# Expert stage of a two-layer decoder kernel: four experts' outputs side by side, weights applied to the output, routing by sort and search

## The reference

```python
def hier_moe_block(x, norm_g, w_rg, b_rg, w_re, b_re, w1, w3, w2):
    xn = rms_norm(x, norm_g).reshape(n_tok, d)                      # 256 tokens x 1024
    g_prob = softmax(xn @ w_rg + b_rg);  g_w, g_idx = top_k(g_prob, 1)          # 1 of 4 groups
    e_logits = (xn @ w_re + b_re).reshape(n_tok, N_GROUPS, EXPERTS_PER_GROUP)
    e_in = take_along_axis(e_logits, g_idx)                         # that group's 8 logits
    e_w, e_idx = top_k(softmax(e_in), 2)                            # 2 of 8 experts
    e_w = e_w / sum(e_w) * g_w
    combine = zeros((n_tok, 32)).at[token, g_idx * 8 + e_idx].add(e_w)
    hid = silu(einsum("nd,edf->nef", xn, w1)) * einsum("nd,edf->nef", xn, w3)   # f = 256
    hid = hid * combine[:, :, None]
    return x + einsum("nef,efd->nd", hid, w2)
```

## Time and profile before

| | |
|---|---|
| median of 3 runs (lowest, highest) | 1025.53 us (1025.33, 1029.95) |
| the profiled execution, its span | 1027.59 us, 1025.6 us |
| PE busy | 965.9 us, 94% |
| DVE, ACT busy | 479.1 us (47%), 466.2 us (45%) |
| DMA | 293.36 MB, mean 286 GB/s |
| TensorE's granted clock, mean | 0.982 of full speed |

### The profile page before, as it was taken

How to read it: one execution, slowest core, us unless ns; L and a number is a source line. 1 busy time by engine, 2 the same in 40 slices (tenths; PEclk the granted TensorE clock), 3 DMA queues, 4 the chain that set the end, 5 groups by cost and what they waited for, 6 DMA issues and landing times.

```text
span 1025.6 us, 19125 instructions
## 1 busy us (share of the span) xinstructions
PE 965.9 (94%) x8018; PEld 784.6 (76%) x8018; DVE 479.1 (47%) x811; ACT 466.2 (45%) x719; POOL 23.7 (2%) x42
## 2 busy tenths in 40 slices
PE   7999999999999999977999999999999899999676
PEld 7898899899886666643598988998998866666344
DVE  6446775567753222211273577654587532222112
ACT  6455555565544333311275464564655443343111
POOL 1010000000000000000000100000000000000000
PEclk9999999999999999988999999999999999999899
DMA  9634544556898999999975246535668799999996
GB/s 301 239 123 164 171 165 164 206 179 233 316 358 313 404 421 419 420 420 420 391 254 177 83 164 187 189 125 205 246 209 358 296 356 408 420 420 420 420 420 255
DMA packets 85478, 293.36 MB, mean 286 GB/s; under 512 B 16976, under 2 KB 17040, under 8 KB 60816
## 3 DMA queue, kind: packets, MB, share of 16 engines
q1 hardware_dynamic: 85392, 292.12, 74.7%
HBM read 291.05 MB, written 1.05 MB: 285 GB/s over the span
## 4 chain that ended last, share of the span: by engine, by line
PE 79%; DMA 11%; DVE 4%; ACT 3%; issue 1%; SPq 1%; POOL 0%; DVEq 0%; ACTq 0%
PE ps_a L775 10%; PE ps_a L777 10%; PE ps_a L776 10%; PE ps_b L1099 8%; DMA units_over_splits<-in_w_dram 8%; PE ps_b L1119 5%; PE ps_a L759 5%; PE ps_b L1178 4%; PE ps_a L761 4%; PE ps_a L760 4%; PE ps_a L1162 4%; DMA units_over_branches<-in_w_dram 3%; PE ps_b L1048 2%; PE ps_b L986 1%; PE ps_b L878 1%
## 5 line engine op out<-in xcount | busy, mean ns | idle before, releaser
L1210 ACT ACTIVATE w_high<-weight_ring 128x1024 fp32r<-128x1024 f32 x166 | 174.8, 1059 | 206.0 <-PE ps_a L777 146.5
L1496 DVE TENSOR_TENSOR w_low<-weight_ring,w_high 128x1024 fp32r<-128x1024 f32 x168 | 202.9, 1225 | 127.2 <-ACT w_high L1210 124.2
L775 PE MATMUL ps_a<-xnT_high,w_high 128*128 128x256 f32 x704 | 201.5, 286 | 1.7 <-DVE xnT_low L1502 1.7
L777 PE MATMUL ps_a<-xnT_high,w_low 128*128 128x256 f32 x704 | 199.5, 283 | 0.0
L776 PE MATMUL ps_a<-xnT_low,w_high 128*128 128x256 f32 x704 | 198.5, 282 | 0.0
L775 PEld LDWEIGHTS ps_a<-xnT_high,w_high 128*128 128x128 f32 x704 | 133.4, 189 | 4.3 <-issue 4.3
L776 PEld LDWEIGHTS ps_a<-xnT_low,w_high 128*128 128x128 f32 x704 | 133.8, 190 | 0.5 <-issue 0.5
L777 PEld LDWEIGHTS ps_a<-xnT_high,w_low 128*128 128x128 f32 x704 | 132.5, 188 | 0.0
L1872 DVE TENSOR_TENSOR y_lo<-ps_b,y_hi 128x512 fp32r<-128x512 f32 x64 | 44.2, 691 | 150.6 <-ACT y_hi L1461 148.6
L1422 ACT ACTIVATE h<-ps_b 128x512 f32<-128x512 f32 x64 | 38.3, 598 | 125.3 <-PE ps_b L1099 125.3
L1178 PEld LDWEIGHTS ps_b<-fold,h 128*128 128x128 f32 x512 | 69.2, 200 | 33.0 <-issue 28.0
(11 more groups left out here) (343 smaller groups left out, 1568.7 us busy)
## 6 DMA issues: line engine op xcount, KB each, us to landing
weight_ring<-in_w_in_dram SPq DMA_DIRECT2D x64, 1024.0 KB, 5.4
units_over_splits<-in_w_dram SPq DMA_DIRECT2D x60, 1024.0 KB, 23.7
units_over_attention<-in_w_dram SPq DMA_DIRECT2D x46, 1024.0 KB, 15.8
weight_ring<-in_w_dram SPq DMA_DIRECT2D x40, 1024.0 KB, 20.7
units_over_branches<-in_w_dram SPq DMA_DIRECT2D x30, 1024.0 KB, 18.6
weight_ring<-in_w_branch_dram SPq DMA_DIRECT2D x12, 1024.0 KB, 5.2
unit_over_gates<-in_w_dram SPq DMA_DIRECT2D x10, 1024.0 KB, 17.9
weight_ring<-in_w_out_dram SPq DMA_DIRECT2D x8, 1024.0 KB, 6.6
```

What stands on the lines that cost most here:

```text
L775: mm(dst, wh, xh, start=row == 0 and s % 2 == 0, stop=False, skip_group_check=True)
L777: last = mm(dst, wl, xh, start=False, stop=row == rows - 1, skip_group_check=True)
L1210: A(mix_buf(whi, i), mix_raw(i), ACT.Copy).then_inc(hi_ready, 1)
L1496: v.tensor_tensor(mix_buf(wlo, i), mix_raw(i), mix_buf(whi, i).bitcast(F32), ALU.subtract).then_inc(lo_ready, 1)
```

## The change

- A group for `outputs` and `scatter` is now four experts. The 128 rows are 4 experts x 32 slots, and the two halves of the contraction are summed in PSUM by a second matmul. It is still 16 matmuls of 32 rows a group, so half as many per expert, and 8 for the scatter. Only the last two groups are pairs as before.
- `select` holds each expert's columns once. `selectT` has four places.
- The slots' weights are one column per group (`ws`), made with matmuls of one column, and are applied as ACT copies `y_hi` and as DVE makes `y_lo`. The multiplication in `hT` goes.
- The list is written by expert. w2 units come four at a time.
- The ring has 19 places, 2 serve once.
- Routing finds each group's eight logits sorted (`max`) and their places (`max_index`), for one tile at a time; the first tile's part is placed earlier.

```diff
+GROUPS = [(e, 4, 1) for e in range(0, NE - 4, 4)] + [(NE - 4, 2, 2), (NE - 2, 2, 2)]
-ONCE_UNITS = (4, 5, 9)
+ONCE_UNITS = (9, 5)
-    t.once = [once_y[:, :], once_XT1[:, :], once_selT[:, :]]
+    t.once = [once_y[:, :], once_XT1[:, :]]
-    t.ring += [split_[i] for i in (0, 3, 1, 4, 2, 5)]
+    t.ring += [split_[0], split_[3], split_[1], split_[4], unit_inputs[:, :], split_[2], split_[5]]
...
+    for e in range(NE):
+        g = GROUP_OF[e]
+        hidden(e)
+        if e == 0:
+            steps.append(("first", 0))
+            selecting.extend((1, piece, 0) for piece in range(2))
+        elif e == 1:
+            steps.append(("first", 1))
+        elif coming and (e % BATCH >= 2 or e % BATCH == 1 and coming[0][0] == BATCHES - 1):
+            gather()
+        if e == 2:
+            steps.append(("first_selT", 0))
+        if e % 4 == 0 and e:
+            outputs(g - 1)
+        elif e % 4 == 1 and e > 4:
+            steps.append(("scatter", GROUP_OF[e - 4]))
+        elif e == NE - 1:
+            outputs(LAST - 1)
+        hidden_T(e)
+        if e == NE - 1:
+            steps.append(("scatter", LAST - 1))
+        select_next()
+    outputs(LAST)
+    steps.append(("scatter", LAST))
...
+            if g == LAST - 1:
+                idle_work(11)
+            for i in range(count):
+                arrived(pe, n + i)
...
+                for turn_j in range(2 // cuts):
+                    for c in range(TILES):
+                        e, j = c // cuts, c % cuts + turn_j
+                        w2 = unit_buf(n + e)[:, j * D + n2 * 512:j * D + (n2 + 1) * 512]
+                        ins = mm(ps_y[c * SLOTS:(c + 1) * SLOTS, n2, :], t.hid[:, (first + e) % 4, j, :], w2,
+                                 start=turn_j == 0, stop=turn_j == 2 // cuts - 1, skip_group_check=True)
...
+                        A(t.yhi[:, n2 * 512:(n2 + 1) * 512], ps_y[:, n2, :], ACT.Copy,
+                          scale=t.ws[:, g:g + 1]).then_inc(yhi_done, 1)
...
+            for g in range(NG):
+                last = v.max(t.tops[:, tt, g, :], rest[:, tt, g, :])
...
+            for g in range(NG):
+                last = v.max_index(t.top_at[:, tt, g, :], t.tops[:, tt, g, :], rest[:, tt, g, :])
```

More of the change, by code:

```diff
@@ L64, with steps_of @@
 TOKEN_MAJOR = {"sbv", "mlv", "mbv", "mbq", "mbk", "if"}
-STEPS = [("rows", q) for q in range(NK // 2)] + [("weights", 0)] + [("select", q) for q in range(2)]
+def steps_of(n):
+    groups = [g for g, (e, _, _) in enumerate(GROUPS) if e // BATCH == n]
+    return ([("rows", q) for q in range(NK // 2)] + [("weights", groups)] +
+            [("select", groups[i:i + 2]) for i in range(0, len(groups), 2)])
 def bc(ap, axis, count):
@@ L486, in hidden_T, with outputs @@
         h_used.append(banks)
[L488 to L493, removed]
-    def gather():
[L497 to L504, removed]
+    def outputs(g):
+        first, count, _ = GROUPS[g]
+        steps.append(("y", (g, len(order))))
+        order.extend(("w2", e) for e in range(first, first + count))
+        used.extend(count * [used[-1] + TILES])
+        y_used.append(used[-1])
+    selecting, y_used = [], []
+    coming = [(n, i, step) for n in range(1, BATCHES) for i, step in enumerate(steps_of(n))]
+    def gather():
+        nonlocal banks
+        n, i, step = coming.pop(0)
+        steps.append(("gather", (n, *step, banks)))
+        banks += 1
+        if i == len(steps_of(n)) - 1 and n + 1 < BATCHES:
+            selecting.extend((n + 1, piece, banks) for piece in range(2))
     def select_next():
@@ L508, in select_next @@
             steps.append(("selection", selecting.pop(0)))
[L510 to L513, removed]
+    for e in range(NE):
+        g = GROUP_OF[e]
+        hidden(e)
+        if e == 0:
             steps.append(("first", 0))
-            selecting.extend((1, piece, 0) for piece in range(3))
-        else:
+            selecting.extend((1, piece, 0) for piece in range(2))
+        elif e == 1:
+            steps.append(("first", 1))
+        elif coming and (e % BATCH >= 2 or e % BATCH == 1 and coming[0][0] == BATCHES - 1):
             gather()
[L518 to L528, removed]
-            steps.append(("first_selT", 0))
[L530 to L536, removed]
+        if e == 2:
+            steps.append(("first_selT", 0))
+        if e % 4 == 0 and e:
[7 more added lines that the diff above has]
+            steps.append(("scatter", LAST - 1))
         select_next()
-    outputs(PAIRS - 1)
-    steps.append(("scatter", PAIRS - 1))
-    assert gathers == (BATCHES - 1) * len(STEPS) and not selecting
+    outputs(LAST)
+    steps.append(("scatter", LAST))
+    assert not coming and not selecting
     ONCE, RING = len(t.once), len(t.ring)
@@ L1813, in first_rows @@
                     ins.then_inc(rows_dve, 1)
-        select(0, 0)
+        select(0)
         low(1)
@@ L1845, in run_vector @@
                     if piece == 0:
-                        dve.wait_ge(*((given, uses) if uses else (first_given, 3)))
-                    if piece < 2:
-                        select(n, piece)
+                        dve.wait_ge(*((given, uses) if uses else (first_given, 2)))
+                        select(n)
                     else:
```

255 lines of the change are left out of this document (114 added, 141 removed).

## The result

| | before | after |
|---|---|---|
| median (lowest, highest), 20 runs each | 1027.42 us (1025.33, 1031.45) | 1031.78 us (1027.92, 1036.74) |
| ratio, 95% interval | | 1.0039 (1.0023 to 1.0054) |
| profiled execution, its span | 1027.59, 1025.6 us | 1031.16, 1029.2 us |
| PE busy | 965.9 us | 939.6 us |

The changed kernel is slower by 0.4%, though PE has 26 us less to do. The prediction was 5.6 us faster.

A forecast was written before the change was run, and what follows sets the result against it. The 420 GB/s weight stream was taken to bound the expert stages. Routing 0.6 plus start 2.6 gave 3.2 us a layer, 6.4 for two, less 0.8 at the end: 5.6 gained, median 1019.9 us, range 1016 to 1026.

The forecast's parts named there:

- What bounds the kernel: Expert stages: the weight stream at 420 GB/s, 2.50 us per unit, sets the stage; 75 streamed units take 187 us.
- PE's work per expert: Expert chain on PE: falls from 1.91 to 1.52 us per unit, worth nothing past 345 us, something at the start.
- Routing: Logits to the end of `assigned`: 2.7 us for 3.32, 0.6 us less a layer; bounds 1.0 less to 1.0 more.
- Start of the stream: First refills of each layer: twelfth lands at 35.5 for 38.5 us, 3.0 sooner; 2.6 us a layer taken.
- The ring: Ring of 19 places for 18: at worst 17 are held, so the DMA isn't stopped; 0 us.
- Output scale: ACT's and DVE's instructions per half keep their size and lie beside PE; 0 us.
- The end: Chain from expert 27's w2 to the last outputs: low clock after longer w2 waits may make it late; 0.8 us lost.
- 0 or 1.5: Second layer's end: chain late by 1.5 us if it starts at low clock, else by 0; 0.8 taken.
- the end runs at half clock: Rival, stage end: 1.2 GHz up to the last landing costs 8.3 us a layer, giving 1035.7 us; chance 0.08.

The follow-up runs named there:

- B: Changed kernel with the first two gather pieces in PSUM banks of their own; median 1025.51 us, 0.9983 of the kernel before.
- the repeat: The changed kernel timed again, unaltered, beside the kernel before on the same chip; median 1031.30 us, ratio 1.0048 to before.
- K: Changed kernel with 18 ring places, the place over the inputs serving once; median 1030.56 us, ratio 1.0026 to before.
- C: Changed kernel without the idle filler matmuls at the last expert and ahead of the outputs; median 1029.64 us, ratio 1.0023 to before.
- H: Changed kernel with the first two gather pieces in own banks and without the end's filler matmuls; median 1024.93 us, ratio 0.9978 to before.
- I: Changed kernel with gather pieces in own banks, no end fillers, and 28 fillers in each of two long w2 waits; median 1026.36 us, ratio 0.9982 to before.
- D: Kernel before, without its filler matmuls at the last expert's w3 half and ahead of the outputs; median 1030.92 us, ratio 1.0038 to before.
- G: Changed kernel without the end's fillers, with four fillers in the bank wait of experts three, four, seven, eight; median 1026.41 us, ratio 0.9990 to before.
- E: Changed kernel with 28 filler matmuls ahead of the sixth and seventh groups' outputs, in the w2 waits; median 1029.61 us, ratio 1.0017 to before.

## Why the prediction was wrong, point by point

- **What bounds the kernel: right.** The stream at 420 GB/s sets the stage, and 26 us less work for PE bought nothing.
- **PE's work per expert: wrong by the outputs, without effect past 345 us.** The prediction has 3.7 us for outputs and scatter of four experts, 1.52 us per unit. The outputs of a group are 32 matmuls and 3.64 us, not 1.85, which makes 1.67 (36.4 + 2 x 1.8, over 24 units). Between 345 and 500 us, 62 units, PE is busy 15.3 us less: 0.25 a unit, close to 1.91 - 1.67, not the 0.39 forecast.
- **Routing: right, a little low.** 0.6 us a layer was forecast, 0.82 and 0.88 came. `max` was 0.09 us as taken. `max_index` was two instructions, of 0.07 to 0.09 and 0.16 us, that overlap: the four took 0.56 us (304.03 to 304.59), 0.14 each for 0.17 taken. The Trainium skill ("Vector Engine (DVE) Microarchitecture Reference", The match/index hardware and the swap-based sort pattern) has it as a load of the values and then the search, and the trace agrees.
- **Start of the stream: the step that failed first.** "Experts 2 and 3 have no outputs and no scatter, so hidden starts at 3.7, 7.3, 11.4, 15.5" took a step to be the sum of its instructions, 1.86 + 1.15 + 1.06. What was left out is that gather and fold share a bank, and that the outputs between them were the cover of ACT's copy. The starts were 3.8, 7.6, 12.8 and 17.9. Behind them the first outputs of four experts took 3.64 us, not 1.85. So the four places came back at + 24.7 instead of + 20.8: by B, 2.5 us of it is the bank, and 1.4 is left, which fits the outputs; no run tests those alone. SP's refills had gaps of 5.2 and 5.6 us, over the 5 that the prediction named as its sign. The twelfth refill landed at + 38.4 instead of + 35.5, and 2.6 us a layer became none. B, which takes the wait away, brings the predicted starts to 0.3 us, and about 2 us of the gain by the rate at the start.
- **What that wait did to the clock: not in the prediction at all.** The low clock was looked for in waits for w2 alone. It fell in the early stretch in some executions, 3.4 us a layer in the profile of the repeat. What it costs a run is an estimate: if the groups of the repeat's times (1030.3, 1032.6, 1036.1, so some 2.9 us apart) count it, it came 8 times in 12 runs, 8 x 2.9 / 12 = 1.9 us on average; by the profiles, 4 of 10 layers with F 3.1 us later, 2 x 0.4 x 3.1 = 2.5 us.
- **The ring: right** (K). Its filling and emptying had no part.
- **Output scale: nearly nothing.** ACT's copy takes 0.69 us for 0.60 and DVE's 0.75 for 0.69. The Trainium skill ("ScalarE: Activation LUTs", What ACT_TABLE_LOAD costs) gives about 93 ns for a per-partition operand, and the trace agrees with 0.09 us. It lies beside PE but for the last outputs: 0.13 us a layer.
- **The end: mechanism right, size wrong.** The prediction had the two lengths, 26.3 and 24.8 us, and the 1.5 between them, but gave layer 1 nothing, because there the last landing had also been 26.3 us behind. That was one execution: its last unit landed 4.16 us after the one before, not 2.49, and hid the lateness. After, the layers had 25.1 and 24.8 us to spend, and 26.5 of chain that began 0.35 us behind the landing. In layer 2 the "0 or 1.5" was halved to 0.8, though after waits of 9 us the low clock was the rule: the profiles of the changed kernel, its repeat, C and K show 10 us of it at each of the last two waits of either layer. It was 1.70 and 1.93. And the 4 us of idle matmuls in that chain were not seen as work of the path: without them (C) the end is on time.

Together: -1.7 (routing) - 0.45 (T0 to F) + 3.45 (end) + 0.4 (scatter and mixer) is + 1.7, and the early clock adds an estimated 1.9 to 2.5 in the mean: + 3.6 to + 4.2. Measured, as a difference of means: + 4.0 in the first 20 runs and + 4.6 in the repeat (of medians, + 4.4 and + 3.5). What the later logits add, up to 1.7 us, is open, so the sum is no proof to a microsecond. Of the rival "the end runs at half clock", the place was right and the price was not: the low level ended at 489.5 us, well before the last units, so the last outputs were 1.7 to 1.9 us late a layer, not 8.3.

What stays open: why the clock fell in the early stretch of some layers and not of others, why it falls near the last landing in H and I, and whether the later logits are chance.

## What to carry to other kernels

When instructions are taken out from between two users of one buffer, ask what they covered: here the copy out of a PSUM bank, 1 us a step, and through the idle time the clock. Price a step by the chain through its buffers, not by the sum of its instructions, and count the matmuls of a merged step in the program before a row of the old one is taken as its price. Matmuls that only keep PE warm must be placed anew with every change of the waits around them, and a chain's slack is to be read in both layers, or several runs, before it is called free.

## What the runs showed of the hardware beside this

- TensorE's granted clock fell not only after waits of 3.94 and 8.9 us, but also where PE was idle 1.02 us in each 5.12. In the same place it did so in one execution of the changed kernel and not in another.
- The fillers at the end of layer 1 cost something far behind it. From layer 1's last scatter to the second layer's logits, the five profiles without them (C, D, G, H, I) show 294.9 to 295.0 us, and the nine with them 296.4 to 296.6. Each of the nine has a stretch of 3.4 us at low clock between 704 and 717 us, and none of the five has. In the first mixer the same place, 101 us ahead of the logits, has it in three profiles (the repeat, E and K, at 200 to 205 us). Why a few idle matmuls at 502 us would do that 200 us later is not shown. It is part of what C gains.
- An unchanged 16-matmul group takes 1.05 us at 2.4 GHz and 1.95 us at 1.2 GHz, but the DMA's loss comes 10 us later, as the places it frees are late (103 GB/s at 336 to 341 us in the repeat).
